# Opening of a two-layer encoder kernel: weights loaded in four parts, rows scaled by their token factor ahead of time, more of the first sums on TensorE

## The reference

```python
mod = c_act @ w_ada[l] + b_ada[l]
shift, scale, gate = jnp.split(mod, 3, axis=-1)
h = _rmsnorm(x, norm_w) * (1.0 + scale[:, None]) + shift[:, None]
proj = h @ w_in
q, k, v, ga, u, gp, z, xbc, dt_raw, gl = jnp.split(proj, ...)
```

## Time and profile before

| | us |
|---|---|
| median of 3 runs | 1134.92 |
| lowest and highest of them | 1134.83, 1135.31 |
| the profiled execution's own time | 1134.01 |
| its span in the profile | 1132.3 |
| PE busy | 1112.1 (98%) |
| DVE, ACT, POOL busy | 660.6, 532.6, 561.7 |

### The profile page before, as it was taken

One profiled execution on the slowest core, in us unless ns is written; L12 is line 12 of the kernel. 1 busy time (PEld: TensorE's weight loads), 2 busy tenths in 40 slices (PEclk: granted clock), 3 DMA queues, 4 the chain that ended last, 5 costly groups with the idle time before them and its releaser, 6 DMA issues.

```text
span 1132.3 us, 15212 instructions
## 1 busy us (share of the span) xinstructions
PE 1112.1 (98%) x5807; PEld 917.6 (81%) x5807; DVE 660.6 (58%) x830; ACT 532.6 (47%) x930; POOL 561.7 (50%) x412
## 2 busy tenths in 40 slices
PE   6999999999999999999999999999999999999997
PEld 5778888888888888888898788888788887888885
DVE  4716465668788545538870635664887854131365
ACT  5544266655545533224462535666546553232234
POOL 5535444535445546545914363445355535464455
PEclk8999999999999999999999999999999999999999
DMA  9656423234443456653304463224433523443332
GB/s 322 208 134 197 132 76 93 76 112 131 129 119 84 129 177 199 206 156 104 96 20 101 142 205 93 76 75 120 130 99 99 132 73 87 116 133 94 105 100 93
DMA packets 203481, 140.79 MB, mean 124 GB/s; under 512 B 12001, under 2 KB 191249, under 8 KB 203409
## 3 DMA queue, kind: packets, MB, share of 16 engines
q1 hardware_dynamic: 202632, 138.91, 42.5%
q10 hardware_dynamic: 776, 0.91, 0.3%
HBM read 136.64 MB, written 2.63 MB: 123 GB/s over the span
## 4 chain that ended last, share of the span: by engine, by line
PE 95%; DVE 2%; SPq 1%; DMA 1%; issue 0%; POOL 0%; ACT 0%; DVEq 0%; POOLq 0%
PE main L683 77%; PE psC L683 6%; PE psA L683 5%; PE psB L683 4%; SPq L398 1%; DMA big<-in_w_ada 1%; PE psB L916 1%; PE psB L896 1%; DVE h_lo L1552 1%; SPq L426 0%; DVE psC L1505 0%; DVE tmp L1547 0%; PE psC L925 0%; POOL tmp L627 0%; DVE tmp L1505 0%
## 5 line engine op out<-in xcount | busy, mean ns | idle before, releaser
L601 POOL TENSOR_TENSOR w_lo<-raw,w_hi 128x512 fp32r<-128x512 f32 x344 | 502.3, 1481 | 537.4 <-ACT w_hi L1101 537.2
L683 PE MATMUL main<-h_hi,w_hi 128*128 128x512 f32 x976 | 388.7, 399 | 3.1 <-ACT h_hi L1101 2.9
L683 PE MATMUL main<-h_hi,w_lo 128*128 128x512 f32 x976 | 379.5, 390 | 0.0
L683 PE MATMUL main<-h_lo,w_hi 128*128 128x512 f32 x976 | 379.3, 390 | 0.0
L1101 ACT ACTIVATE w_hi<-raw 128x512 fp32r<-128x512 f32 x344 | 199.9, 623 | 286.1 <-PE main L683 161.8
L683 PEld LDWEIGHTS main<-h_hi,w_hi 128*128 128x128 f32 x976 | 183.6, 188 | 49.4 <-issue 11.1
L683 PEld LDWEIGHTS main<-h_hi,w_lo 128*128 128x128 f32 x976 | 183.2, 188 | 38.9
L683 PEld LDWEIGHTS main<-h_lo,w_hi 128*128 128x128 f32 x976 | 183.3, 188 | 38.0 <-issue 1.9
L1874 DVE TENSOR_TENSOR tmp<-main,misc 128x512 f32<-128x512 f32 x32 | 22.1, 692 | 165.3 <-PE main L683 162.8
L1713 DVE SCALAR_TENSOR_TENSOR misc<-main,cols,misc 128x511 f32<-128x511 f32 (+2 forms) x96 | 71.9, 749 | 60.9 <-ACT misc L1101 58.3
L683 PE MATMUL main<-y_hi,w_hi 128*128 128x512 f32 x256 | 100.5, 393 | 0.0
(11 more groups left out here) (288 smaller groups left out, 1411.8 us busy)
## 6 DMA issues: line engine op xcount, KB each, us to landing
raw<-in_w_in SPq DMA_DIRECT2D x124, 512.0 KB, 3.9
xbc<-in_w_ada SPq DMA_DIRECT2D x16, 512.0 KB, 4.9
zs<-in_w_ada SPq DMA_DIRECT2D x16, 512.0 KB, 4.6
raw<-in_w_pc SPq DMA_DIRECT2D x16, 512.0 KB, 3.8
raw<-in_w_out SPq DMA_DIRECT2D x16, 512.0 KB, 3.6
zs<-in_w_ada SPq DMA_DIRECT2D x16, 256.0 KB, 7.6
xbc<-in_w_in SPq DMA_DIRECT2D x8, 512.0 KB, 7.6
big<-in_w_ada SPq DMA_DIRECT2D x16, 256.0 KB, 7.2
```

Of the source, the lines that this page charges most:

```text
L601: nc.gpsimd.tensor_tensor(lo_b[:, cut, :], raw_b[:, cut, :], hi_b[:, cut, :].bitcast(F32), ALU.subtract).then_inc(s_split[b], 2 * BT_ // kt)
L683: return nc.tensor.matmul(o, a, b_, start=start, stop=stop)
```

## The change

1. The weights of the wide tiles come in four parts of two blocks (`wide(part)`), one behind each quarter. A part is two DMAs: couple 0 in 1 KB rows, and couples 1 and 2 together in 2 KB rows. ACT makes three high parts per part (`wide_hi_part`), POOL three low parts (`split_wide`); each takes both tiles of a couple for two blocks, so each is as large as before (128 x 512), and there are 12 on each engine as before.
2. Blocks 0 to 3 are multiplied by the token factor ahead (`x_scale`, DVE, in place). For them ACT then makes `h_hi` directly from `xT` with `mod` as scale and bias (`h_high_first`) and no longer waits for DVE's fp32 product, which `h_32_first` makes beside it. The low parts of blocks 0 and 1 move from DVE to POOL.
3. In quarter 0 PE sums slab 4 too (`slab_sums`), and DVE three slabs where it did four behind the root.
4. `quarter_sums` adds the offsets `b_ada` by one more product with the identity; `quarter_mod` has two instructions where it had three.
5. Behind `quarter_sums(0)` PE makes two fp32 products of 256 columns that nobody reads.
6. ACT's scaled slabs of quarter 2 are parted: two ahead of blocks 2 and 3, two behind.

The DMAs of quarter 2 wait for the new counts of used slabs, `load` of the fourth couple waits for the low part of couple 0's last part, and counts in waits are shifted. The diff, without these counts:

```diff
@@ -71,7 +71,7 @@
-BY_PE = (2, 3)
+BY_PE = (2, 3, 4)
@@ -307,7 +308,9 @@
-            xbc[:, KT + 4 * i:KT + 4 * i + 4, :].rearrange("p a (k n) -> p (a k) n", n=2 * P) for i in range(2)]
+            xbc[:, KT:CT, i * 2 * P:(i + 1) * 2 * P] for i in range(2)]
+        couple_hi, couple_lo = ([h[:, :, :, :]] + [t[:, 4 * i:4 * i + 4, :].rearrange("p (b a) (k n) -> p b (a k) n", b=2, n=P)
+                                                   for i in range(2)] for h, t in ((w_hi, y_hi), (w_lo, y_lo)))
...
         def tokens(half):
@@ -406,8 +407,7 @@
             def load(l, u, b, w, col, kt=KT):
...
-                    for e in range(2):
-                        sp.wait_ge(s_split[e], part_count(0, 0, 1, e))
+                    sp.wait_ge(s_splitw, couple_count(0, KT - 1))
@@ -419,21 +419,18 @@
-            def wide(half):
-                cut = slice(half * BT_, (half + 1) * BT_)
-                for u in range(U_GA):
-                    sp.dma_start(couple_raw[u][:, cut, :], w_in_t[0, :, cut, u * 2 * P:(u + 1) * 2 * P]
-                                 ).then_inc(s_rawx[u][half], 16)
+            def wide(part):
+                cut = slice(2 * part, 2 * part + 2)
+                sp.dma_start(couple_raw[0][:, cut, :], w_in_t[0, :, cut, 0:2 * P]).then_inc(s_rawx[part], 16)
+                sp.dma_start(xbc[:, KT + 2 * part:KT + 2 * part + 2, :], w_in_t[0, :, cut, 2 * P:6 * P]
+                             ).then_inc(s_rawx[part], 16)
...
-            quarter(0)
-            wide(0)
-            quarter(1)
-            quarter(2)
-            wide(1)
-            quarter(3)
+            for q in range(QUARTERS):
+                quarter(q)
+                wide(q)
@@ -601,11 +598,20 @@
+            def split_wide(part):
+                cut = slice(2 * part, 2 * part + 2)
+                for u in range(U_GA):
+                    pool.wait_ge(s_hiw, couple_count(u, 2 * part))
+                    nc.gpsimd.tensor_tensor(couple_lo[u][:, :, cut, :],
+                                            couple_raw[u][:, cut, :].rearrange("p k (b n) -> p b k n", b=2),
+                                            couple_hi[u][:, :, cut, :].bitcast(F32), ALU.subtract).then_inc(s_splitw, 1)
             def split_pre(i):
...
-                pool.wait_ge(s_hiw, i + 1)
+                pool.wait_ge(s_hiw, couple_count(U_GA - 1, KT - 1) + i + 1)
@@ -628,14 +634,16 @@
-                    for u, b in WIDE[:5]:
-                        split_half(l, u, b, 0)
-                    add_products(1)
-                    split_half(l, 2, 1, 0)
-                    add_products(2)
-                    for u, b in WIDE:
-                        split_half(l, u, b, 1)
-                    add_products(3)
+                    for q in range(QUARTERS):
+                        split_wide(q)
+                        if q < QUARTERS - 1:
+                            add_products(q + 1)
+                        if q == 0:
+                            for k in range(2):
+                                pool.wait_ge(s_h32, k + 1)
+                                pool.wait_ge(s_hhi, k + 1)
+                                nc.gpsimd.tensor_tensor(h_lo[:, k], h_tmp[k], h_hi[:, k].bitcast(F32), ALU.subtract
+                                                        ).then_inc(s_h, 1)
@@ -775,15 +783,22 @@
-                    last = mm(quarter_ps[q][:, j:j + 1], quarter_acc[q % 2][:, j * P:(j + 1) * P],
-                              ones[:, 0:1], q > 0, q > 0 or j == QUARTERS - 1)
-                last.then_inc(s_adam, 1)
+                    mm(quarter_ps[q][:, j:j + 1], quarter_acc[q % 2][:, j * P:(j + 1) * P], ones[:, 0:1],
+                       q > 0 and j == 0, False)
+                pe.wait_ge(s_cols, 1)
+                mm(quarter_ps[q], ident[:, :],
+                   cols[:, 0, V_BADA:V_BADA + 2 * KT].rearrange("p (w k) -> p w k", w=2)[:, :, 2 * q:2 * q + 2], False, True
+                   ).then_inc(s_adam, 1)
...
             def first_rows():
...
-                pe.wait_ge(s_ada[BY_PE[0] // 2], 32)
-                for k in BY_PE:
+                slab_sums(BY_PE[:2])
+            def slab_sums(ks):
+                for k in ks:
+                    pe.wait_ge(s_ada[k // 2], 32)
@@ -827,26 +841,24 @@
             def wide_pair(q):
...
-                tiles = range(len(WIDE) - 1 if q == 0 else len(WIDE))
...
-                wide_low_weights(a, tiles)
+                wide_low_weights(a)
...
-                wide_low_weights(b, tiles)
+                wide_low_weights(b)
...
-                for k in (a, b):
-                    wide_low_weights(k, range(len(tiles), len(WIDE)))
...
             def wide_end(i, k0):
...
+                pe.wait_ge(s_splitw, couple_count(u, k0))
@@ -863,8 +875,11 @@
+            slab_sums(BY_PE[2:])
...
-            pe.wait_ge(s_cols, 1)
+            pe.wait_ge(s_xca, 2)
+            for _ in range(2):
+                mm(psB[:, 512:768], ident[:, :], x_tok[:, 0, 0:256])
...
             for q in range(QUARTERS - 1):
@@ -1113,12 +1128,20 @@
+            def wide_hi_part(part):
+                cut = slice(2 * part, 2 * part + 2)
+                for u in range(U_GA):
+                    act.wait_ge(s_rawx[part], 32)
+                    f(couple_hi[u][:, :, cut, :], couple_raw[u][:, cut, :].rearrange("p k (b n) -> p b k n", b=2), ACT.Copy
+                      ).then_inc(s_hiw, 1)
             def pre_hi(i):
...
-                act.wait_ge(s_rawx[u][half], 32)
+                act.wait_ge(s_rawx[2 * u + half], 48)
@@ -1181,13 +1204,19 @@
+            def h_high_first(k):
+                act.wait_ge(s_mod, k // 2 + 1)
+                act.wait_ge(s_xs, k + 1)
+                f(h_hi[:, k, :], xT[:, k, :], ACT.Identity, scale=mod[:, 0, KT + k:KT + k + 1], bias=mod[:, 0, k:k + 1]
+                  ).then_inc(s_hhi, 1)
             def h_high(l, k, half=0, tok=slice(0, SEQ)):
...
-            def products(q):
-                for k in range(OWN[q]):
+            def products(q, ks=None):
+                for k in ks or range(OWN[q]):
@@ -1197,21 +1226,20 @@
-            for u, b in WIDE[:4]:
-                w_hi_half(0, u, b, 0)
-            h_high(0, 0)
-            h_high(0, 1)
-            w_hi_half(0, 2, 0, 0)
-            w_hi_half(0, 2, 1, 0)
+            wide_hi_part(0)
+            h_high_first(0)
+            h_high_first(1)
...
-            products(2)
-            h_high(0, 2)
-            h_high(0, 3)
-            for u, b in WIDE:
-                w_hi_half(0, u, b, 1)
+            wide_hi_part(1)
+            products(2, range(2))
+            h_high_first(2)
+            h_high_first(3)
+            products(2, range(2, OWN[2]))
+            wide_hi_part(2)
...
+            wide_hi_part(3)
@@ -1538,8 +1566,25 @@
             def quarter_mod(q):
+                k0, k1 = 2 * q, 2 * q + 2
...
-                modulation(0, quarter_ps[q], 2 * q, 2 * q + 2)
+                stt(mod[:, 0, KT + k0:KT + k1], quarter_ps[q][:, 2:4], 1.0, cols[:, 0, V_NORM + k0:V_NORM + k1], ALU.add,
+                    ALU.mult)
+                nc.vector.tensor_copy(mod[:, 0, k0:k1], quarter_ps[q][:, 0:2]).then_inc(s_mod, 1)
+                dve.wait_ge(s_mod, q + 1)
+            def x_scale(k):
+                tt(xT[:, k], xT[:, k], psC0, ALU.mult).then_inc(s_xs, 1)
+            def h_32_first(k):
+                dve.wait_ge(s_xs, k + 1)
+                ts_(h_tmp[k], xT[:, k], mod[:, 0, KT + k:KT + k + 1], mod[:, 0, k:k + 1], ALU.mult, ALU.add
+                    ).then_inc(s_h32, 1)
+            def h_low_first(k):
+                dve.wait_ge(s_hhi, k + 1)
+                dve.wait_ge(s_h, k)
+                tt(h_lo[:, k], h_tmp[k], h_hi[:, k].bitcast(F32), ALU.subtract).then_inc(s_h, 1)
...
             def h_32(l, k, half=0, tok=slice(0, SEQ), ps=psC0):
@@ -1584,23 +1629,33 @@
-            use_rows(0, ((2, 4), (3, 5), (4, 6), (5, 7)))
+            use_rows(0, ((2, 5), (3, 6), (4, 7)))
+            dve.wait_ge(rms[3], 1)
+            dve.wait_ge(s_xc, 2)
+            dve.wait_ge(s_xca, 2)
+            x_scale(0)
             for q in range(QUARTERS):
...
-                    dve.wait_ge(rms[3], 1)
-                    dve.wait_ge(s_xc, 2)
-                    dve.wait_ge(s_xca, 2)
-                h_32(0, 2 * q)
-                h_32(0, 2 * q + 1)
-                own = tuple((k - OWN[q + 1], k) for k in range(OWN[q + 1], KT)) if q < QUARTERS - 1 else ()
-                use_rows(q + 1, own[:-1] if q == 0 else own)
-                h_low(0, 2 * q)
-                h_low(0, 2 * q + 1)
+                    x_scale(1)
+                for k in (2 * q, 2 * q + 1):
+                    if q < 2:
+                        h_32_first(k)
+                    else:
+                        h_32(0, k)
...
-                    use_rows(q + 1, own[-1:])
+                    x_scale(2)
+                    x_scale(3)
+                if q < QUARTERS - 1:
```

(42 more changed lines are left out.)

1 line of the change is left out of this document (added).

## The result

| us | before | after |
|---|---|---|
| median, on one chip | 1134.70 (20 runs) | 1137.29 (20 runs) |
| lowest and highest | 1134.13, 1135.31 | 1135.81, 1138.69 |
| the profiled execution's own time | 1134.01 | 1136.47 |
| its span | 1132.3 | 1134.6 |

The ratio of after to before is 1.0022, with a 95% interval of 1.0016 to 1.0028: the changed kernel is slower by 2.6 us. The forecast of 1136.5 was a shift of 1.6 us from the 1134.92 of the first three runs. The range held the time; the most likely case, within 0.2%, was just missed, as 0.22% lies on the far side of a bound that the interval straddles. Profile against profile the difference is 2.46 us.

A forecast was written before the change was run, and what follows sets the result against it. Bound: when the opening reaches `wide_end`, PE alone thereafter. Terms -0.8, -1.8, -0.45, +0.2, +1.8 and -0.2 follow the lead to +1.7 by the schedule; +1.6 taken, 1136.5 us against the median 1134.92; range 1132.6 to 1138.2.

The forecast's parts named there:

- the most likely case: Whole kernel: a time within 0.2% (2.27 us) of before, 1132.65 to 1137.19 us, chance 0.70.
- rival C: Opening: clock rises only at 25.4 to 26.2 us, PE late at second sums; +2.2 to +2.6, 1137.4 us, chance 0.20.
- The bound: Opening up to `wide_end` at 52.80 us: only a shift of that moment counts; PE's earlier start is worth nothing by itself.
- Quarter 0: First sums: end at 19.2 us as before; first wide product at 20.7 us, 0.8 earlier, despite 1.7 us of unread products.
- The clock's rise: PE's opening: full clock 4.74 us after dense products begin at 19.0, so at 23.8 us instead of 26.22.
- Quarters 1 and 2: Second pair at 31.4 us instead of 34.27; POOL's additions end at 35.8, third pair's rows begin at 41.0: lead gone.
- Rival D: Opening: the change does less than it says; POOL's late low parts of blocks 0 and 1 cost little; within forecast's range.
- Quarter 3: DVE's low parts of blocks 4 and 5 beside POOL's splits: 3.3 us instead of 1.4, 1.8 lost; `wide_end` at 54.8.
- Rival A: DVE and POOL lose little by taking turns; `wide_end` 1.35 us before the old 53.1, 1133.6 us, chance 0.18.
- Rival B: Up to `wide_end`, PE is the bound if additions are ready in time: 3.0 us early, 1131.9 us, chance 0.10.
- Nothing later takes this back or adds: Behind `wide_end`: the shift of 1.7 us goes unchanged to the end; later-issued loads still land in time.

The follow-up runs named there:

- Experiment 1: The changed kernel with the last part of the weights loaded, rounded and split ahead of quarter 3's slabs instead of behind: 1136.32 us, ratio 1.0015.
- experiment 5: The kernel before with three unread 128x512 additions on POOL behind those of quarter 3: 1136.35 us, ratio 1.0017.
- experiment 2: The changed kernel with quarter 2's sums on PE behind the low weights of block 3 instead of ahead: 1136.9 us, ratio 1.0021.
- experiment 6: experiment 3 with one slab each of quarters 2 and 3, or of quarter 2 alone, summed by PE: 1134.62 and 1134.63 us.
- experiment 3: The changed kernel with the edits of Experiment 1 and experiment 2 together: 1135.49 us, ratio 1.0008.
- experiment 7: The kernel before with offsets added by TensorE and two unread products: 1135.48 us; offsets alone 1136.34; unread products alone 1135.19.

## Why the prediction was right, and what it missed

The steps up to `wide_end` came out near their forecasts one by one. The range was wide: from 1132.6 to 1138.2 us, it holds the time of before as well, so that it held says little. And 1137.29 is nearer to rival C's 1137.4 than to the forecast's 1136.5, though it did not come by C's path.

**The bound** (right). `wide_end` was the moment to look at, and PE's earlier start was worth nothing by itself: PE is 0.73 us earlier at the first wide product and 3.12 us earlier at the second pair, and 1.75 us later at the end.

**Quarter 0** (right in sum). The sums start at 17.10 and the first wide product at 20.75, forecast 20.7. The two unread products hold PE for 1.5 us net, 0.2 less than the estimate and within its bounds.

**The clock's rise** was put at 23.8 and came at 22.2. Rival C did not come about, but its price was right: without the products, where the clock rises late, the shift is 2.3 against "+2.2 to +2.6", and PE comes to the second sums at 30.3 us. From there it went on through ACT's slab and POOL's additions, though, and not through DVE's slabs as C had it. The Trainium skill's statement that the point varies from run to run ("TensorE: Matmul & The Clock Gate", Part 1) agrees with the two pairs of profiles of one kernel: 22.2 and 22.7, 25.9 and 25.7. Over all profiles it lies between 22.1 and 24.8 us in the nine with the products, and between 25.1 and 26.8 in the five without them, so one execution with them can have it 2.7 us later than another.

**Quarters 1 and 2** (right). The second pair starts at 31.15, forecast 31.4. POOL is done with the additions of quarter 2 at 36.16, forecast 35.8; DVE's fp32 rows of blocks 0 and 1 took 2.06, forecast 2.2; PE waits 2.37 us, forecast 1.9; the third pair of rows begins at 41.02, forecast 41.0. The whole lead is gone there, as written.

**Rival D** (the change does less) was bounded rightly. POOL's low parts of blocks 0 and 1 end at 27.95, 1.4 us later than written. Most of that is a slip of the sum: three splits, two additions and two low parts from 18.3 us on come to 27.4 by the forecast's own prices, not 26.5. PE still waits for nothing between 20.75 and the third sums.

**Quarter 3** (right, and shown). The two low parts take 3.23 us instead of 1.41, forecast 3.3; they end at 50.27 and 51.94, forecast 50.3 and 52.1, with POOL's last split in between (51.39), so POOL did not win every turn; `wide_end` starts at 54.55, forecast 54.8. Experiment 1 takes the splits away and the shift goes in the profile, though only 0.7 us of the median; experiment 5 puts three instructions of that kind into the kernel before and 2.0 us come, in the profile and in the median. Rival A (turns cost little) is out by both.

**Rival B, PE as the bound**, did not come about for after, but PE had only 0.33 us left at `wide_end`. What brought it there was the fall of the clock behind the third sums, which no step had. It costs nothing in the changed kernel (experiment 2 has no fall and the same time). That it costs the kernels that mend the rest what they would win is an estimate (experiments 1 and 6).

**The step that failed** is the sentence "Nothing later takes this back or adds". The shift of 1.75 is the 1.7 of the schedule, and 1136.5 would have followed from it; in the profiled execution what comes on top is one later wait of 0.88 us: PE at 107 us for a low part whose load takes 5 or 6 us, behind which the kernel before had nothing to spare. The rows to see it by were in the trace of before: the product at 104.64 us starts 0.14 us after POOL's split ended. The distance of 0.33 us to the product ahead of it alone would not have told, as dozens of other products of that trace start 0.29 us or more after the one ahead with no wait between. They were not looked at, since the chain of waits shows PE alone there. No experiment gave that load more time, so this is read from the profiles and not tried; it remains open what share of the median it is, and the other profile of the same kernel has no wait there.

## What to carry to other kernels

An instruction that runs while its engine has nothing else to do is not free if it works in SBUF beside one that the end waits for: look at what each moved instruction will stand beside, on the other engine, before counting it as covered.

An engine that arrives earlier at a wait gains nothing and may lose: in several profiles PE's idle time ahead of the sums was followed by a half clock that then had to be worked off. And "PE is alone from here on" is a reading of one execution: look for products that start just when what they need has ended on another engine, since these are waits with no slack, which turn a change in the length of a load into time. And one profile is one execution: of experiment 1 it was nearly the fastest, of experiment 3 the slowest.

## What was not expected of the hardware

- The granted clock falls to 1.2 GHz in mid-kernel, in eight of the fourteen profiles, for about 3.4 us each time, in which two products take 1.05 us instead of 0.62. Ahead of the sums that it fell behind PE had idled 2.37 and 2.30 us (the changed kernel, twice), 1.26 and 1.27 (without the unread products), 0.97 (experiment 3), 1.43 (the unread products in before), 0.46 with sixteen one-column products, and nothing with sixteen (experiment 6). It did not fall behind 1.66 us (experiment 1), nor behind 1.44 and 1.31 us (experiment 7, with both and with the offsets). So the idle time alone does not tell; what does was not found.
- The edits widened the spread of the runs: 1.2 us for before with 20 runs and 1.5 to 1.6 with 31 to 33, but 2.9 us for after and 3.6 us for experiment 1, where only the work of the first 55 us differs.
- A load of 0.5 MB at 99.1 us took 5.1 us to land in one execution and 6.0 in another, of the same kernel.
